# Gated DeltaNet tiles: decay matrix in its own buffer, a tile's output finished after the next tile's Gram products, v copied unscaled, no state work in tile 0; GLA output matmuls grouped by shape

## The chip, the cores and the metric

The kernel runs on one core of a Trainium2 chip. The metric is the device time of one execution in microseconds; three executions are known for the kernel before. Engines are named as in the profile: PE is the matmul engine (TensorE; PEld is its weight loads), DVE is VectorE, ACT is ScalarE, POOL is GpSimd, SP only issues DMAs.

## The reference

Two layers of `x + W_out[concat_g(mixer_g(h) * silu(z_g))]` with `h = RMSNorm(x)`, 512 tokens, width 2048. One input projection of 7192 columns feeds four mixers with 4 heads each: GLA, sliding-window attention, differential attention and gated DeltaNet (GDN). The change touches GDN and the output of GLA.

```python
# GDN, chunks of C = 64 tokens, d = 128
qc = l2_norm(ch(q)) * d ** -0.5 ; kc = l2_norm(ch(k)) ; vc = ch(v)
dec = jnp.cumsum(g, axis=-1)
dmask = jnp.where(tril, jnp.exp(dec_i - dec_j), 0.0)
M = jnp.where(strict, (kb @ kc.T) * dmask, 0.0)      # kb = kc * beta
Tm = inverse(M + eye)
u = Tm @ (vc * beta) ; w = Tm @ (kb * exp(dec))
...
def step(S, inp):
    v_new = u_n - w_n @ S
    o_n = qd_n @ S + qk_n @ v_new
    S = S * dl_n + ke_n.T @ v_new
# S starts at zero; then o = rms_norm(o, norm_g), times silu(z)
# GLA, chunks of 64:
o = a @ vc + q_dec @ S_prev                          # o_intra + o_inter
```

## The kernel before

**Projection as the carrier.** PE multiplies in a split form: each weight block is held as a rounded high half (`w_hi`, a DMA that POOL issues) and the rest (`w_lo`, computed by POOL in line 399). One step ("kt") of `project` (line 414) is 12 matmuls of 128x512 in line 438, three for each of four accumulators `acc[0..3]` in PSUM. A chunk of 512 columns is 16 such steps. After a chunk the four accumulators are read out by `take_out` (ACT, line 881), and the first matmul of the next chunk into `acc[b]` waits for `acc_free`.

**Mixer work between projection steps.** The mixers are Python generators; at fixed places inside a chunk (`k`, `b` odd) `project` takes one stage of a generator. So the order of PE's instructions is written out: no scheduler moves anything. GDN has four tiles of 128 tokens (`t` = 0..3), 18 stages each, spread as 8 stages in chunk `dz` and 16 in each of `bz`, `az`, `aq`, `av`. Stages of one tile on PE:
- stage 1: `gap` (line 486: the decay matrix `AG` times a triangle, into PSUM bank 3) and `nat` (line 490: transposes of q, k, v into banks 0, 1, 2);
- stage 2: the Gram products `kk`, `kq` (line 498);
- stages 3 to 14: six levels of the triangular inverse, each a `y` stage (line 506) and a `q` stage (line 522). Between them ACT copies Y (line 994) and DVE updates X (line 1361);
- stages 15 to 18: the last blocks of the inverse and the state products `ks`, `qs` (line 541), then `pt`, `tr`, and `s`, `o` (lines 562, 565).

**ACT and DVE** run the same tiles in their own program order, tied by counting semaphores (`Steps`). For each tile ACT does squares (982, 983), the exponential of the decays (984), Ln and Exp for the norms (986 to 989, each with a table load ahead), the six copies, the gate, and at the end the output's square (1010), Ln and Exp (1012, 1014). `GDN_STAGES` also sets where ACT's `take_out` calls stand among its stages: after 8, 24, 40, 56 and 72. DVE computes `ke`, `red`, `cq`, `nb`, `ei`, `nt0..3`, `qk`, then `r` (line 1351, v times 1/norm), `xi` (line 1352, the identity into X), the levels, and at the end of the tile `o` (1383), `redo` (1385), `mo` (1387), the four output products `y0..3` (1391), and only then `decayed(t + 1)` (1328), which builds `AG` of the next tile. `AG` shares its place with `QK`, and the `o` products read `QK`:

```python
U = dict(..., KE=unit(9, 0), AG=unit(9, 1), QK=unit(9, 1), ...)
def decayed(t):
    if t:
        dve.wait_ge(D_PE.sem, D_PE.at(l, f"{t-1}.o"))
    dve.tensor_tensor(U["AG"], heads(after_all), cols(glog[:, t]), ALU.mult)
```

**GLA** has one tile per chunk in the four chunks after GDN, six stages each. Its last stage makes, for each head, one 128-row product (line 624) and two 64-row products (line 628) into the same PSUM columns.

Of the kernel before, what the change touches and what calls it, by code (L numbers as in the profile page):

```python
# [23 lines left out]
EPS = 1e-6  # L24
# [60 lines left out]
def names(fmt, *ranges):  # L85
# [10 lines left out]
GDN_PE = "gap nat kk kq y1 q1".split() + [f"{a}{lv}" for lv in LV for a in ("y", "tx", "q")] + \  # L96
    "fin y7 ks qs pt tr s o".split()
GDN_ACT = "sqq sqk ex lnk rk irk".split() + [f"y{lv}" for lv in range(1, LEVELS + 1)] + \
    "gate y7 tt0 tt2 sqo lno ro".split()
GDN_DVE = "ag ke red cq nb ei nt0 nt1 nt2 nt3 qk r xi x1".split() + [f"{a}{lv}" for lv in LV for a in ("xt", "x")] + \  # L100
    "tt1 g3 rn0 rn1 rn2 rn3 qs w s0 s1 s2 s3 o redo mo y0 y1 y2 y3".split()
# [17 lines left out]
def hybrid_trunk(nc, x, wstream, wsmall, pcol, prow, wlr, cf, masks, out):  # L119
    ctx = ExitStack()  # L120
    with ctx:
# [81 lines left out]
        U = dict(S=unit(8, 0), R=unit(8, 1), W=unit(8, 2), QS=unit(8, 3), KE=unit(9, 0), AG=unit(9, 1), QK=unit(9, 1),  # L203
# [75 lines left out]
        def lay(prefix, *parts):  # L279
# [11 lines left out]
                                                                    "glog", "gA", "zero_tt", "zero_gdn"] +  # L291
# [4 lines left out]
        D_PE = Steps(sem("gdn_pe"), names("", T, GDN_PE))  # L296
        D_ACT = Steps(sem("gdn_act"), names("", T, GDN_ACT))
        D_DVE = Steps(sem("gdn_dve"), names("", T, GDN_DVE))
# [107 lines left out]
        def _(pe):  # L406
# [47 lines left out]
            def gdn(l):  # L454
# [11 lines left out]
                for t in T:  # L466
# [87 lines left out]
                    dve_at("rn3")  # L554
# [14 lines left out]
            def gla(l, t):  # L569
# [51 lines left out]
                for h in H:  # L621
                    b, p = slice(DK * (h % 2), DK * (h % 2) + DK), h // 2
                    o = mh[3 if h % 2 else 1]
                    nc.tensor.matmul(o[:, h], V["AT"][:, h], slot(SLOT["av"])[:, t, HD * h:HD * h + HD],
                                     start=True, stop=False)
                    for j in range(2):
                        r = slice(CH * j, CH * j + CH)
                        last = nc.tensor.matmul(o[r, h], V["QKT"][b, P * p + CH * j:P * p + CH * j + CH],
                                                V["S"][b, (2 * t + j) % 3, p], start=False, stop=True)
# [240 lines left out]
        def _(act):  # L870
# [57 lines left out]
            for l in range(DEPTH):  # L928
# [13 lines left out]
                def conv_gate(c):  # L942
# [32 lines left out]
                    .then_inc(S_ACT.sem, S_ACT.one("decs"))  # L975
                def gdn():

                    for t in T:
# [5 lines left out]
                        nc.scalar.activation(U["EX"], mh[3], ACT.Exp).then_inc(*s("ex"))  # L984
                        w(D_DVE, "red")
# [4 lines left out]
                        yield  # L990
                        yield
# [190 lines left out]
        def _(dve):  # L1182
# [57 lines left out]
            for l in range(DEPTH):  # L1240
# [81 lines left out]
                dve.memset(U["S"], 0.0).then_inc(*si("zero_gdn"))  # L1322

                def decayed(t):

                    if t:
                        dve.wait_ge(D_PE.sem, D_PE.at(l, f"{t-1}.o"))
                    dve.tensor_tensor(U["AG"], heads(after_all), cols(glog[:, t]), ALU.mult) \
                        .then_inc(D_DVE.sem, D_DVE.one(f"{t}.ag"))

                decayed(0)
                for t in T:
# [6 lines left out]
                    dve.tensor_scalar(sc, ss[:, 0:4], EPS, EPS * HD, ALU.add, ALU.mult).then_inc(*s("cq"))  # L1339
# [11 lines left out]
                    dve.tensor_tensor(U["R"], mh[2], cols(rs[:, 8:12]), ALU.mult).then_inc(*s("r"))  # L1351
                    dve.tensor_copy(X, ident_half.unsqueeze(1).broadcast_to([P, HEADS, CH])).then_inc(*s("xi"))
                    w(D_DVE, "xi")
                    for lv in range(1, LEVELS + 1):
                        if lv > 1:
# [8 lines left out]
                            .then_inc(*s(f"x{lv}"))  # L1364
                    w(D_PE, "fin")
# [274 lines left out]
```

## Time and profile before

| what | value |
|---|---|
| median of 3 executions | 2056.3 us (2053.81 to 2058.85) |
| profiled execution, its own time | 2057.32 us |
| its span, first to last instruction | 2055.5 us |
| PE busy | 1969.5 us (96%) |
| DVE, ACT, POOL busy | 659.5, 518.3, 919.7 us |
| chain that ended last | PE 83% of the span, 68% in line 438 alone |
| mean granted TensorE clock | 0.984 of full speed |

The profiled execution's time is its span plus 1.8 us around it, and lies 1.0 us above the median. The busy time of PE counts matmuls whose ends are modelled; starts are what the text uses.

### The profile page before, as it was taken

How to read it: one execution, taken by the hardware profiler on the slowest of the kernel's cores; microseconds unless marked ns; L12 is line 12 of the kernel's file. 1: busy time of each engine (PE TensorE's matmuls, PEld its weight loads, DVE VectorE, ACT ScalarE, POOL GpSimd, SP SyncE). 2: the span in 40 equal slices, each digit the busy share in tenths (PEclk: the TensorE clock that was granted, in tenths of full speed). 3: DMA queues.
4: the chain of work that ended last, by engine and by line, in shares of the span. 5: the costliest groups of instructions: out<-in, count | busy, mean ns of one | idle time of the engine just before them, and what ended most of it. 6: DMA issues, size and time to landing. Idle time of an engine off the chain costs nothing.

```text
span 2055.5 us, 26277 instructions
## 1 busy us (share of the span) xinstructions
PE 1969.5 (96%) x10984; PEld 1586.3 (77%) x10984; DVE 659.5 (32%) x1252; ACT 518.3 (25%) x1014; POOL 919.7 (45%) x876
## 2 busy tenths in 40 slices
PE   7999988989999999999999999989999999999999
PEld 5887777777888878777888877777778887786787
DVE  1545123122111343443324462232221113425433
ACT  4111122022222444322321011221222225533220
POOL 4455433433555444344555544333434444433454
PEclk9999999999999999999999999999999999999999
DMA  8565544544555544645775655434445555464466
GB/s 273 156 189 166 146 118 120 144 123 124 164 164 164 164 139 144 209 133 160 216 222 155 194 154 144 123 112 135 135 129 165 165 164 162 127 213 128 151 172 197
DMA packets 92181, 326.95 MB, mean 159 GB/s; under 512 B 10174, under 2 KB 10912, under 8 KB 91040
## 3 DMA queue, kind: packets, MB, share of 16 engines
q0 software_dynamic: 41472, 151.01, 26.4%
q1 hardware_dynamic: 44288, 155.75, 25.4%
q10 hardware_dynamic: 6304, 18.52, 2.3%
q8 instruction: 87, 1.43, 0.3%
q14 instruction: 30, 0.25, 0.0%
HBM read 316.86 MB, written 8.39 MB: 158 GB/s over the span
## 4 chain that ended last, share of the span: by engine, by line
PE 83%; DVE 8%; ACT 7%; issue 1%; DMA 1%; SPq 0%; ACTq 0%; DVEq 0%
PE acc L438 68%; PE mix L710 1%; PE mix L490 1%; DVE slots L1288 1%; PE mix L506 1%; PE mix L522 1%; ACT L1074 1%; ACT L1071 1%; PE mix L729 1%; PE mix L541 1%; PE mix L688 1%; PE mix L802 1%; PE mix L512 1%; PE mix L757 1%; DMA slots<-in_x 1%
## 5 line engine op out<-in xcount | busy, mean ns | idle before, releaser
L399 POOL TENSOR_TENSOR w_lo<-w_raw,w_hi 128x512 fp32r<-128x512 f32 x576 | 754.3, 1310 | 790.6 <-DMA w_hi<-in_wstream 506.0
L438 PE MATMUL acc<-w_hi,actT_hi 128*128 128x512 f32 x1920 | 788.1, 410 | 9.8 <-ACT slots L881 9.3
L438 PE MATMUL acc<-w_hi,actT_lo 128*128 128x512 f32 x1920 | 754.5, 393 | 0.0
L438 PE MATMUL acc<-w_lo,actT_hi 128*128 128x512 f32 x1920 | 753.0, 392 | 0.0
L438 PEld LDWEIGHTS acc<-w_hi,actT_hi 128*128 128x128 f32 x1920 | 365.0, 190 | 101.1 <-issue 28.8
L438 PEld LDWEIGHTS acc<-w_hi,actT_lo 128*128 128x128 f32 x1920 | 362.7, 189 | 79.3
L438 PEld LDWEIGHTS acc<-w_lo,actT_hi 128*128 128x128 f32 x1920 | 365.2, 190 | 66.1
L381 POOL DMA_DIRECT2D w_hi<-in_wstream x288 | 163.7, 568 | 335.0 <-PE acc L438 330.8
L438 PE MATMUL acc<-actT_hi,w_hi 128*128 128x512 f32 x384 | 152.6, 397 | 0.0
L438 PE MATMUL acc<-actT_hi,w_lo 128*128 128x512 f32 x384 | 150.1, 391 | 0.0
L438 PE MATMUL acc<-actT_lo,w_hi 128*128 128x512 f32 x384 | 150.0, 391 | 0.0
L438 PEld LDWEIGHTS acc<-actT_hi,w_lo 128*128 128x128 f32 x384 | 72.4, 188 | 15.4
L438 PEld LDWEIGHTS acc<-actT_hi,w_hi 128*128 128x128 f32 x384 | 72.5, 189 | 15.0 <-issue 0.5
L438 PEld LDWEIGHTS acc<-actT_lo,w_hi 128*128 128x128 f32 x384 | 72.4, 189 | 14.9 <-issue 0.5
L994 ACT ACTIVATE slots<-mix 128x256 f32<-128x256 f32 x48 | 18.5, 385 | 250.4 <-PE mix L506 250.4
L1508 DVE TENSOR_TENSOR slots<-acc,slots 128x512 f32<-128x512 f32 x64 | 43.6, 692 | 88.6 <-PE acc L438 88.6
L948 ACT ACTIVATE general<-slots 128x512 f32<-128x512 f32 x24 | 15.2, 633 | 211.7 <-DVE slots L1288 211.7
L1288 DVE SCALAR_TENSOR_TENSOR slots<-slots,pcol_all 128x511 f32<-128x511 f32 (+2 forms) x72 | 67.2, 933 | 2.5
L1361 DVE COPY_PREDICATED slots<-mask_sb,mix 128x256 f32<-128x256 uint8 x48 | 21.5, 448 | 143.7 <-PE mix L522 143.7
L881 ACT ACTIVATE slots<-acc,xr 128x512 f32<-128x512 f32 x56 | 36.9, 688 | 90.8 <-PE acc L438 90.8
L1357 DVE COPY slots<-mix 128x256 f32<-128x256 f32 x40 | 17.0, 425 | 124.8 <-PE mix L512 124.8
L1404 DVE SCALAR_TENSOR_TENSOR slots<-mix,slots 128x256 f32<-128x256 f32 x8 | 3.4, 424 | 155.4 <-ACT slots L1032 155.4
(247 smaller groups left out, 1754.6 us busy)
## 6 DMA issues: line engine op xcount, KB each, us to landing
w_hi<-in_wstream POOLq DMA_DIRECT2D x288, 512.0 KB, 3.9
w_raw<-in_wstream SPq DMA_DIRECT2D x288, 512.0 KB, 4.5
out_x<-slots ACTq DMA_DIRECT2D x7, 1024.0 KB, 8.0
slots<-in_x SPq DMA_DIRECT2D x4, 1024.0 KB, 15.6
slots<-in_x ACTq DMA_DIRECT2D x1, 4096.0 KB, 16.8
slots<-out_x ACTq DMA_DIRECT2D x1, 4096.0 KB, 16.3
out_x<-slots ACTq DMA_DIRECT2D x4, 256.0 KB, 2.2
cf_sb<-in_cf ACTq DMA_DIRECT2D x1, 933.0 KB, 11.2
```

The source lines that it names most:

```text
L381: pool.dma_start(w_hi[:, g % HI].rearrange("p a n -> p (a n)"), wstream[g:g + 1].rearrange("a p n -> p (a n)")).then_inc(hi_in[g % HI], 16)
L399: pool.tensor_tensor(w_lo[:, n % RING], w_raw[:, g % RAW, k], w_hi[:, g % HI, k].bitcast(F32), ALU.subtract).then_inc(w_ready, 1)
L438: last = nc.tensor.matmul(acc[b][:, :], lhsT, rhs, start=(k == 0 and i == 0), stop=(k == kts - 1 and i == 2))
L490: last = nc.tensor.transpose(mh[i][:, h], s[:, h, cs], ident)
L506: last = nc.tensor.matmul(y_out[rs_, j, gs], U["NT"][js, h, js], X[js, h] if lv > 1 else ident_half[js, :], start=True, stop=True)
L512: last = nc.tensor.transpose(mix[1][:, P * g:P * g + P], X[:, 2 * g:2 * g + 2].rearrange("p h c -> p (h c)"), ident)
L522: last = nc.tensor.matmul(p_out[js, r, gs], XT[rs_, g, js] if lv > 1 else ident_half[rs_, :], Y[rs_, j, gs], start=True, stop=True)
L541: last = nc.tensor.matmul(mh[i][:, h], s[:, h, cs], U["S"][:, h], start=True, stop=True)
L881: nc.scalar.activation(slot(SLOT[c])[:, b], acc[b][:, :], ACT.Copy, scale=r) \
L1288: dve.scalar_tensor_tensor(dst[:, d:], src[:, 0:SEQ - d], tap[i], dst[:, d:], ALU.mult, ALU.add).then_inc(*ci(f"t{i}"))
L1361: dve.copy_predicated(X_by_r, m_x[lv - 1].rearrange("p (g c) -> p g c", g=2).unsqueeze(1) .broadcast_to([P, 2, 2, CH]), p_out.rearrange("p ...
L1508: dve.tensor_tensor(xs, acc[b][:, :], xs, ALU.add).then_inc(acc_free, 1)
```

## The change

- `AG` gets its own place (`unit(7, 0)`), and `decayed(t + 1)` is issued before the `w` step of tile t instead of after its output.
- The tail of a tile's output (`redo`, `mo`, `y0..3` on DVE; Ln and Exp on ACT) goes into `gdn_out(t)` and `out_scale(t)`, issued in the next tile: on DVE after `xi`, on ACT after the norms' Exp and before the first Y copy. For the last tile they stand behind all stages and, on ACT, behind `take_out` of `av`.
- ACT copies v out of PSUM unscaled (step `v`); DVE scales it (`r`) in SBUF after the first level. PE's first `y` stage waits for `xi` and `v`, before for `r`.
- Tile 0 has no `ks`, `qs` products and no state terms; the zeroing of S goes.
- GLA's last stage makes the four 128-row products first and then the eight 64-row ones.

```diff
-        U = dict(... KE=unit(9, 0), AG=unit(9, 1), QK=unit(9, 1),
+        U = dict(... KE=unit(9, 0), AG=unit(7, 0), QK=unit(9, 1),
...
-                        dve_at(f"x{lv-1}" if lv > 1 else "r")
+                        dve_at(f"x{lv-1}" if lv > 1 else "xi")
+                        if lv == 1:
+                            act_at("v")
...
-                    if t == 0:
-                        pe.wait_ge(S_DVE.sem, S_DVE.at(l, "zero_gdn"))
-                    for i, s, step in ((0, k, "ks"), (1, q, "qs")):
+                    for i, s, step in ((0, k, "ks"), (1, q, "qs")) if t else ():
...
                 for h in H:
+                    nc.tensor.matmul(mh[3 if h % 2 else 1][:, h], V["AT"][:, h],
+                                     slot(SLOT["av"])[:, t, HD * h:HD * h + HD], start=h < 2, stop=False)
+                for h in H:
                     b, p = slice(DK * (h % 2), DK * (h % 2) + DK), h // 2
                     o = mh[3 if h % 2 else 1]
-                    nc.tensor.matmul(o[:, h], V["AT"][:, h], slot(SLOT["av"])[:, t, HD * h:HD * h + HD],
-                                     start=True, stop=False)
...
+                def out_scale(t):
+
+                    act.wait_ge(D_DVE.sem, D_DVE.at(l, f"{t}.mo"))
+                    nc.scalar.activation(sa, sa, ACT.Ln).then_inc(D_ACT.sem, D_ACT.one(f"{t}.lno"))
+                    act.wait_ge(D_ACT.sem, D_ACT.at(l, f"{t}.lno"))
+                    nc.scalar.activation(sa, sa, ACT.Exp, scale=-0.5).then_inc(D_ACT.sem, D_ACT.one(f"{t}.ro"))
...
+                        nc.scalar.activation(U["R"], mh[2], ACT.Copy).then_inc(*s("v"))
...
                         yield
+                        if t:
+                            out_scale(t - 1)
                         yield
...
                     take_out(l, c)
+                out_scale(TILES - 1)
...
-                dve.memset(U["S"], 0.0).then_inc(*si("zero_gdn"))
...
-                    dve.tensor_tensor(U["R"], mh[2], cols(rs[:, 8:12]), ALU.mult).then_inc(*s("r"))
                     dve.tensor_copy(X, ident_half.unsqueeze(1).broadcast_to([P, HEADS, CH])).then_inc(*s("xi"))
+                    if t:
+                        gdn_out(t - 1)
...
+                        if lv == 1:
+                            dve.scalar_tensor_tensor(U["R"], U["R"], 1.0 if t else -1.0, cols(rs[:, 8:12]),
+                                                     ALU.mult, ALU.mult).then_inc(*s("r"))
...
+                    if t + 1 < TILES:
+                        decayed(t + 1)
                     w(D_PE, "tr")
                     dve.tensor_tensor(U["W"], mh[0], cols(sd), ALU.mult).then_inc(*s("w"))
...
+                    else:
+                        dve.tensor_copy(U["S"], mh[2]).then_inc(*s("s"))
...
-                    if t + 1 < TILES:
-                        decayed(t + 1)
+                gdn_out(TILES - 1)
```

What ACT's order is around the start of tile 3, layer 0, before (982 to 984 read the transposes; 986 to 989 are the norms with a table load ahead of each function; 881 is `take_out` of `aq`; 994 are the Y copies):

```order
L982 ACTIVATE slots<-mix 128x512
L983 ACTIVATE slots<-mix 128x512
L984 ACTIVATE general<-mix 128x512
L986 ACT_TABLE_LOAD
L986 ACTIVATE stat<-stat,eps_t 128x4
L988 ACT_TABLE_LOAD
L988 ACTIVATE stat<-stat 128x4
L989 ACTIVATE stat<-stat 128x4
L881 ACTIVATE slots<-acc,xr 128x512 x4
L994 ACTIVATE slots<-mix 128x256 x6
```

The same stretch of the changed kernel (1018 to 1020 are the old 982 to 984, 1021 is the copy of v, 1023 to 1026 the norms, 1008 and 1010 are `out_scale` of tile 2, 910 is `take_out`, 1033 the Y copies):

```order
L1020 ACTIVATE general<-mix 128x512
L1021 ACTIVATE slots<-mix 128x512
L1023 ACT_TABLE_LOAD
L1023 ACTIVATE stat<-stat,eps_t 128x4
L1025 ACT_TABLE_LOAD
L1025 ACTIVATE stat<-stat 128x4
L1026 ACTIVATE stat<-stat 128x4
L1008 ACT_TABLE_LOAD
L1008 ACTIVATE stat<-stat 128x4
L1010 ACT_TABLE_LOAD
L1010 ACTIVATE stat<-stat 128x4
L910 ACTIVATE slots<-acc,xr 128x512 x4
```

Ln and Exp of tile 2's output, with two table loads, now stand between tile 3's norms and the read-out of chunk `aq`.

DVE at the end of tile 1 and the start of tile 2, before (1376 is `w`, 1379 the state, 1383 `o`, 1385 `redo`, 1387 `mo`, 1391 `y0..3`, 1328 the next `AG`, 1336 and 1337 `ke` and `red` of the next tile):

```order
L1376 TENSOR_TENSOR slots<-mix,stat 128x512
L1379 SCALAR_TENSOR_TENSOR slots<-slots,decs,mix 128x128 x4
L1383 TENSOR_TENSOR slots<-mix,slots 128x512
L1385 TENSOR_REDUCE stat<-slots 128x4
L1387 SCALAR_TENSOR_TENSOR stat<-stat 128x4
L1391 SCALAR_TENSOR_TENSOR slots<-slots,stat 128x128 x4
L1328 TENSOR_TENSOR slots<-cf_sb,glog 128x512
L1336 TENSOR_TENSOR slots<-mix,decs 128x512
```

The same stretch of the changed kernel (1361 is the next `AG`, 1434 `w`, 1438 the state, 1445 `o`; 1385 to 1401 are the next tile's `ke` to `xi`; 1370, 1372, 1377 are `redo`, `mo`, `y0..3` of the tile before; 1412 is the first update of X):

```order
L1361 TENSOR_TENSOR slots<-cf_sb,glog 128x512
L1434 TENSOR_TENSOR slots<-mix,stat 128x512
L1438 SCALAR_TENSOR_TENSOR slots<-slots,decs,mix 128x128 x4
L1445 TENSOR_TENSOR slots<-mix,slots 128x512
...
L1401 COPY slots<-cf_sb 128x256
L1370 TENSOR_REDUCE stat<-slots 128x4
L1372 SCALAR_TENSOR_TENSOR stat<-stat 128x4
L1377 SCALAR_TENSOR_TENSOR slots<-slots,stat 128x128 x4
L1412 COPY_PREDICATED slots<-mask_sb,mix 128x2x2x64
```

`AG` has moved ahead of `w`, and the output's tail has moved from the end of its tile to behind `xi` of the next.

## Rows read from the trace of the kernel before

**Rows 1.** Waits of PE and of DVE: in total, times, longest, all in us.
```profile
PE mix L486 <- DVE slots L1328: 31.0, 8, 4.5
DVE slots L1376 <- PE mix L556: 51.0, 8, 6.4
```

**Rows 2.** Timeline of PE, tile 0 to 1, layer 0: start, length, what, idle before.
```profile
262.66 0.39 PE L438 MATMUL acc<-w_hi,actT_lo 128*128 128x512 f32 x1
267.57 1.51 PE L486 MATMUL mix<-cf_sb,slots 128*128 128x128 f32 x8 [4.52 <-DVE slots L1328]
268.87 2.77 PE L490 MATMUL mix<-cf_sb,slots 128*128 128x128 f32 x12
271.29 0.61 PE L438 MATMUL acc<-w_hi,actT_hi 128*128 128x512 f32 x1
...
279.73 0.46 PE L506 MATMUL mix<-cf_sb,slots 64*64 64x64 f32 x16 [0.78 <-DVE slots L1351]
```

**Rows 3.** Timeline of DVE, same stretch.
```profile
260.50 0.68 DVE L1383 TENSOR_TENSOR slots<-mix,slots 128x512 f32<-128x512 f32 x1
...
262.60 1.29 DVE L1387 SCALAR_TENSOR_TENSOR stat<-stat 128x4 f32<-128x4 f32 x1
...
266.74 0.68 DVE L1328 TENSOR_TENSOR slots<-cf_sb,glog 128x512 f32<-128x512 f32 x1
...
279.50 0.42 DVE L1352 COPY slots<-cf_sb 128x256 f32<-128x256 f32 x1
```

**Rows 4.** Windows: busy time (instructions) of PE, PEld, DVE, ACT, POOL; granted clock; DMA.
```profile
726.10:728.10 2.00, 2.00 (x13) 1.82 (x14) 0.83 (x4) 0.00 (x0) 0.88 (x1) 1.00 0.81 236
268.90:271.20 2.30, 2.30 (x12) 2.30 (x11) 0.00 (x0) 0.00 (x0) 0.00 (x0) 0.50 0.00 0
```

**Rows 5.** Timeline of PE: a short wait in layer 0's attention part.
```profile
726.10 1.13 PE L688 MATMUL mix<-slots 128*128 128x128 f32 x8 [1.28 <-DVE slots L1489]
```

**Rows 6.** Timeline of ACT and PE around the first take-out behind GDN.
```profile
486.22 0.63 ACT L1010 ACTIVATE slots<-slots 128x512 f32<-128x512 f32 x1 [8.85 <-DVE slots L1383]
...
490.55 2.41 ACT L881 ACTIVATE slots<-acc,xr 128x512 f32<-128x512 f32 x4
...
491.36 0.76 PE L438 MATMUL acc<-w_hi,actT_hi 128*128 128x512 f32 x1 [4.67 <-ACT slots L881]
...
496.61 0.51 PE L438 MATMUL acc<-w_hi,actT_hi 128*128 128x512 f32 x1
```

**Rows 7.** Chain that ended last: a long run of projection matmuls, start, length, count.
```profile
90.34 74.36 PE acc L438 x327
```

**Rows 8.** Timeline of PE: products ks and qs of tile 0, layer 0.
```profile
246.53 2.05 PE L541 MATMUL mix<-slots 128*128 128x128 f32 x16
```

**Rows 9.** Timeline of ACT, start of tile 1, layer 0.
```profile
273.27 1.28 ACT L986 ACT_TABLE_LOAD   x1
274.64 0.30 ACT L986 ACTIVATE stat<-stat,eps_t 128x4 f32<-128x4 f32 x1
```

**Rows 10.** Timeline of POOL at the end of tile 0, layer 0.
```profile
262.58 1.28 POOL L399 TENSOR_TENSOR w_lo<-w_raw,w_hi 128x512 fp32r<-128x512 f32 x1
```

**Rows 11.** Timeline of ACT and PE at the start of chunk av, tile 3.
```profile
426.41 2.40 ACT L881 ACTIVATE slots<-acc,xr 128x512 f32<-128x512 f32 x4
...
427.48 0.39 PE L438 MATMUL acc<-w_hi,actT_hi 128*128 128x512 f32 x1
```

**Rows 12.** Timeline of DVE and PE at the start of tile 0, layer 0.
```profile
191.12 0.48 DVE L1322 MEMSET slots<- 128x512 f32 x1
...
192.49 1.52 PE L486 MATMUL mix<-cf_sb,slots 128*128 128x128 f32 x8 [1.94 <-DVE slots L1328]
```

**Rows 13.** Timeline of PE: GLA tile 0, layer 0.
```profile
521.00 0.67 PE L615 MATMUL mix<-slots 64*64 64x128 f32 x16
...
527.18 0.38 PE L624 MATMUL mix<-slots,general 128*128 128x128 f32 x2
...
530.22 0.50 PE L438 MATMUL acc<-w_hi,actT_hi 128*128 128x512 f32 x1
```

More of the change, by code:

```diff
@@ L95, with gdn_pe, gdn_act, gdn_dve @@
 LV = range(2, LEVELS + 1)
[L96 to L101, printed above, removed]
+LV = range(2, LEVELS + 1)
+def gdn_pe(t):
+    return "gap nat kk kq y1 q1".split() + [f"{a}{lv}" for lv in LV for a in ("y", "tx", "q")] + ["fin", "y7"] + \
+        (["ks", "qs"] if t else []) + "pt tr s o".split()
+def gdn_act():
+    out = []
+    for t in T:
+        out += [f"{t}.{x}" for x in "sqq sqk ex v lnk rk irk".split()]
+        if t:
+            out += [f"{t-1}.lno", f"{t-1}.ro"]
+        out += [f"{t}.y{lv}" for lv in range(1, LEVELS + 1)] + [f"{t}.{x}" for x in "gate y7 tt0 tt2 sqo".split()]
+    return out + [f"{TILES-1}.lno", f"{TILES-1}.ro"]
+def gdn_dve():
+    end = "redo mo y0 y1 y2 y3".split()
+    out = ["0.ag"]
+    for t in T:
+        out += [f"{t}.{x}" for x in "ke red cq nb ei nt0 nt1 nt2 nt3 qk xi".split()]
+        if t:
+            out += [f"{t-1}.{x}" for x in end]
+        out += [f"{t}.x1", f"{t}.r"] + [f"{t}.{a}{lv}" for lv in LV for a in ("xt", "x")] + [f"{t}.tt1", f"{t}.g3"]
+        if t:
+            out += [f"{t}.{x}" for x in "rn0 rn1 rn2 rn qs".split()]
+        if t + 1 < TILES:
+            out += [f"{t+1}.ag"]
+        out += [f"{t}.w"] + ([f"{t}.s{h}" for h in range(3)] if t else []) + [f"{t}.s", f"{t}.o"]
+    return out + [f"{TILES-1}.{x}" for x in end]
 GLA_PE = "u cum dec tr a us o".split()
@@ L295, in hybrid_trunk @@
         CONV_ACT = Steps(sem("conv_act"), [f"{c}{b}" for c in ("dq", "dk", "dv") for b in range(4)])
-        D_PE = Steps(sem("gdn_pe"), names("", T, GDN_PE))
-        D_ACT = Steps(sem("gdn_act"), names("", T, GDN_ACT))
-        D_DVE = Steps(sem("gdn_dve"), names("", T, GDN_DVE))
+        D_PE = Steps(sem("gdn_pe"), [f"{t}.{x}" for t in T for x in gdn_pe(t)])
+        D_ACT = Steps(sem("gdn_act"), gdn_act())
+        D_DVE = Steps(sem("gdn_dve"), gdn_dve())
         A_PE = Steps(sem("gla_pe"), names("", T, GLA_PE))
@@ L1321, in _, with gdn_out @@
                 dve.memset(U["TT"], 0.0).then_inc(*si("zero_tt"))
-                dve.memset(U["S"], 0.0).then_inc(*si("zero_gdn"))
                 def decayed(t):
-                    if t:
-                        dve.wait_ge(D_PE.sem, D_PE.at(l, f"{t-1}.o"))
                     dve.tensor_tensor(U["AG"], heads(after_all), cols(glog[:, t]), ALU.mult) \
                         .then_inc(D_DVE.sem, D_DVE.one(f"{t}.ag"))
+                def gdn_out(t):
+                    w = lambda st, s: dve.wait_ge(st.sem, st.at(l, f"{t}.{s}"))
+                    s = lambda step: (D_DVE.sem, D_DVE.one(f"{t}.{step}"))
+                    gz = slot(SLOT["dz"])[:, t].rearrange("p (h c) -> p h c", h=HEADS)
+                    w(D_ACT, "sqo")
+                    dve.reduce_sum(ss[:, 8:12], U["SQO"], AX.X).then_inc(*s("redo"))
+                    w(D_DVE, "redo")
+                    dve.scalar_tensor_tensor(sa, ss[:, 8:12], 1.0 / HD, (sc, se)[t % 2], ALU.mult, ALU.add) \
+                        .then_inc(*s("mo"))
+                    w(D_ACT, "ro")
+                    w(D_DVE, "g3")
+                    for h in H:
+                        dve.scalar_tensor_tensor(gz[:, h], U["QS"][:, h], sa[:, h:h + 1], gz[:, h],
+                                                 ALU.mult, ALU.mult).then_inc(*s(f"y{h}"))
                 decayed(0)
```

55 lines of the change are left out of this document (26 added, 29 removed).

## The prediction

> **What bounds the kernel now.** The profile's first part says that PE is busy for 96% of the span and DVE, ACT and POOL for less than half, and the chain that ended last is 83% PE. So PE's own program sets the time, and an edit counts only if it takes instructions from PE or changes how long PE waits or at which clock it runs. I therefore read PE's waits next. The largest is line 486, the first product of a GDN tile, behind DVE's line 1328, which builds `AG`: 31.0 us in 8 waits [rows 1]. The timeline shows one of the six between tiles: last projection matmul at 262.66, next PE instruction at 267.57 [rows 2]. What PE waits for there is the whole tail of tile 0 on DVE and ACT: `o` done at 261.18, `mo` at 262.60, the new `AG` from 266.74 [rows 3]. The time is more than the 4.52 us of idleness, because the clock falls: the products and transposes behind the wait run at a granted 0.50, that is 1.2 GHz [rows 4]; behind the wait of 1.28 us at 726.10 [rows 5] it stays at 1.00 [rows 4]. The same happens once per layer behind GDN: PE waits 4.67 us for ACT to read out chunk `av`, which stands behind the output's Ln and Exp, and the next twelve wide matmuls take from 491.36 to 496.61 [rows 6], 5.25 us, where twelve at full clock take 12 x 74.36/327 = 2.73 [rows 7].
>
> **Between tiles (t = 1, 2; both layers).** I count from c, the start of the last projection matmul before the tile (262.66). Before, the first `y` stage starts at 279.73 = c + 17.1 [rows 2]. After, `AG` is long there: DVE makes it in the gap ahead of `w`, where it waits 6.4 us for PE in every tile [rows 1], so its 0.68 us [rows 3] cost nothing; without that gap they would be 0.68 per tile. PE also waits for `o` of the tile before; it ended at 261.18 [rows 3] and PE is ready at c + 0.23 = 262.89, so 1.7 us to spare. Stage 1 then runs at full clock: 8 products at the rate of `ks`, `qs` (16 in 2.05 us, 0.24 of it the modelled end of the last [rows 8]), 0.9 us, and 12 transposes in half of what they took at clock 0.50, (271.29 - 268.87)/2 = 1.21 [rows 2]. The next projection matmul starts at f = c + 2.34.
>
> From f to the first `y` stage the chain is ACT and DVE, not PE: before, 279.73 - 271.29 = 8.44. The copy of v delays the norms' table load by its issue distance of 0.5 us; the Ln behind it started at 274.64 though its table was there at 274.55 [rows 9], so 0.4 of it comes through. `r` leaves the chain: -0.60 (a 128x512 operation of 0.68 whose successor starts 0.60 later). But PE now waits for the end of `xi`, 279.92, where it waited for `r`, about 279.58: +0.34 [rows 3]. Sum +0.14, so 8.6, and `y1` starts at c + 10.95 instead of c + 17.1. Gain 6.1 us per tile, four tiles: **-24.5**. PE still waits some 1.2 us ahead of `y1`; going by [rows 4, 5] the clock stays up.
>
> **The tail in its new place.** On DVE: `xi` ends at about f + 8.5, `redo` 0.7, `mo`. `mo` took 1.29 us [rows 3] although it is 128x4; POOL's `w_lo` subtraction ran from 262.58 to 263.86 [rows 10], and `mo` ended at 263.89. The Trainium skill (SBUF — State Buffer, "SBUF: two separate sides") says that a DVE operation with two SBUF inputs and a GpSimd operation exclude each other for a whole instruction; the trace agrees. By the page `mo` would be short here only if no `w_lo` subtraction runs. The rows leave about 0.2 (my estimate; on ACT an operation of this size takes 0.30 [rows 9]) to 1.29. I take 0.2, since a subtraction of 1.28 per projection step of 2.73 leaves POOL's port free for more than half of the time, and keep the other end. Then Ln 0.2, table load 1.28 [rows 9], Exp 0.2: done at f + 11.05. The Ln's own table load passes while ACT waits. The first Y copy ends at f + 11.4; PE wants it one stage after `y1`, f + 8.6 + 3.3 = f + 11.9 (twelve wide matmuls and 16 small ones). So no wait, or 0.6 per tile with the long `mo`: 0 to +2.5, taken 0. `y0..3` (1.1 us) end by f + 13.3 at worst; X's first update is wanted at f + 15.2. Covered; without cover 1.1 per tile.
>
> **Tile 3.** Here the order of ACT matters: `take_out` of chunk `aq` comes behind the 56th stage, and there `out_scale(2)` now stands ahead of it. Before, the read-out began at 426.41 and its first 0.69 ended before PE wanted `acc[0]` at 427.48 [rows 11]; queued behind it are PE's whole next chunk and the `y` stage. Now: Exp ends f + 11.05, the first of four read-outs (0.6 to 0.7) f + 11.65, PE gets on at f + 11.8. It was ready at f + 2.7 + 1.7 + 1.4 = f + 5.9 (12 matmuls, 16 products, 6 matmuls): a new wait of about 5.9 us. It is longer than the 4.67 of [rows 6], so I let 12 wide matmuls run at half clock as there. Six of them (2.6) stand before `y1`: f + 14.4 = c + 16.75, before about c + 17.0; and the rest of the slow stretch adds 1.4. Tile 3 so gains nothing: +1.1 per layer, **+2.2**. Bounds: +1.1 more per layer with the long `mo`, 1 less if the clock comes back sooner.
>
> **Tile 0.** PE waits 1.94 us for the memset of S and `AG` behind it [rows 12]; the memset's 0.48 go. A wait of 1.45 is nearer to the 1.28 that kept the clock than to 1.94, which did not keep it. If it is kept, stage 1 takes 2.1 instead of about 3.7 (as from 267.57 to 271.29 [rows 2]). 0.5 + 1.6 less 0.14 is 1.9 per layer, bounds 0.3 and 1.9; I take 1.7: **-3.4**. `ks` and `qs` go: 2.05 - 0.24 - 0.1 for the turn back = 1.7 per layer [rows 8]: **-3.4**.
>
> **Behind GDN.** ACT's `take_out` of `av` now follows the square that ends at 486.85 [rows 6]. Its first read-out of 0.69 ends at 487.54, PE starts 0.12 later (as 491.36 stands to 490.55 + 0.69), and the twelve matmuls end by 490.5 instead of 496.61: 6.1 per layer, **-12.2**. If the remaining wait of 1.1 us still brings the half clock, 2.5 less per layer. The last `out_scale` then waits for the read-out and two table loads, and its `y3` ends about 493.5, some 2 us later than before; GLA's first product, which waits for it, stands 36 projection matmuls in, at 487.7 + 8.2 = 495.9. Covered by 2.4 us; without cover up to 2 per layer.
>
> **GLA output.** The last stage runs from 527.18 to 530.22 [rows 13], 3.04 us for 8 + 16 instructions. Ordered by shape, the eight take 0.9 and a turn of 0.1, and 16 of 64 rows take 0.6, as line 615 does just before with the same kind (0.67 with its modelled end) [rows 13]. 1.45 per tile, 8 tiles: **-11.5**. The other end is that the narrow ones keep their present pace of 0.36 per four: -0.7 each, -5.5.
>
> **Sum.** -24.5 + 2.2 - 3.4 - 3.4 - 12.2 - 11.5 = -52.8 against the profiled execution's 2057.3 us: 2004.5. The median of three lies 1.0 lower: **2003.5 us**.
>
> **Rivals.**
> - *The clock.* The waits of 1.2 us ahead of `y1`, with no long gap between tiles any more, are followed by half clock: twelve matmuls at double time, 2.5 us, in 6 places: +15, 2018.5. For it: 1.94 was enough. Against: 1.28 was not. Chance 0.12.
> - *Tile 3 escapes.* PE's wait for the read-out is hidden and tile 3 gains like tiles 1 and 2: -14.4, 1989. Against it: the order shown on ACT leaves no way round, and ACT's Ln cannot start before `xi`. Chance 0.04.
> - *A slower switch of tables.* Each table load holds ACT for another length of itself: +1.3 at tile 3's read-out, +0.8 at each first Y copy: +5.8, 2009. Against: Ln started 0.09 after its load's end [rows 9]. Chance 0.04. The Trainium skill (ScalarE: Activation LUTs, "What ACT_TABLE_LOAD costs") has such a rule, a drain of about 1.38 us with each load; in this trace it does not show.
> - *Slower than before.* PE falls to half clock at the wait ahead of `y1` and stays there through the inverse's levels, whose small products and short waits fill it less than before. Every wide matmul at half clock costs 0.2 us; it decides from 52.8/0.2 = 264 of them, 33 in each of 8 tiles (a tile has 216). All of them would give +340, half a tile each +170, about 2175. Against: before, the same levels ran at full clock, and at 0.984 on average. Chance 0.03.
> - *Nothing happens*, since PE still waits for `o` of the tile before: it had 1.7 us to spare. Then only tile 0, the end and GLA count. Within 0.3% needs more failures still: 0.02.
>
> **How the numbers follow.** My forecast has 0.75, with its own range 1996 to 2011. The slower table switch (2009) lies in it; to 2017 it takes in part of the clock's case. Range 1995 to 2017. Differences under 0.3% (6 us) count as none. Faster 0.95, same 0.02, slower 0.03.
>
> **What would show it.** PE's waits: line 486 behind DVE gone for t > 0, about 1.4 us left for t = 0; a wait of about 1.2 us ahead of each `y1` but tile 3's; two new waits of 5 to 7 us for `take_out` in chunk `av`, clock 0.50 behind them; the wait of 4.67 us down to about 1.1. GLA's last stage 1.6 us. The prediction is wrong if half clock follows short waits, or if the narrow GLA products keep their pace.

## The result, and the profile after

| | before | after |
|---|---|---|
| median of four executions | 2056.84 us (2053.81 to 2058.85) | 2000.89 us (1998.3 to 2004.94) |
| profiled execution, its time | 2057.32 us | 2004.94 us |
| its span | 2055.5 us | 2002.9 us |
| mean granted TensorE clock | 0.984 | 0.993 |

The ratio after to before is 0.9731, 95% interval 0.9708 to 0.9754: the changed kernel is 2.7% faster. The forecast was 2003.5 us. The profiled execution is the slowest of its four; the tables below go by it, and its forecast was 2004.5 us.

The page of the changed kernel, parts 1 and 4: busy time by engine, and the chain that ended last by engine.

```profile
PE 1938.3 (97%) x10952; PEld 1564.2 (78%) x10952; DVE 652.0 (33%) x1234; ACT 521.7 (26%) x1022; POOL 921.4 (46%) x876
...
PE 85%; ACT 7%; DVE 6%; issue 1%; DMA 1%; SPq 0%; ACTq 0%; DVEq 0%
```

PE's waits after, in the columns of [rows 1] (total, times, longest). Line numbers have moved: 466 is the projection (438 before), 514 the `gap` products (486), 536 the first `y` stage (506), 910 ACT's `take_out` (881), 717 an attention product (688), 739 another (710).

```profile
PE acc L466 <- ACT slots L910: 13.0, 4, 5.6
PE mix L717 <- DVE slots L1543: 11.0, 6, 2.7
PE mix L739 <- DVE slots L1577: 7.5, 2, 3.8
PE mix L536 <- DVE slots L1401: 6.7, 6, 1.1
PE mix L514 <- DVE slots L1361: 5.2, 2, 2.8
```

Line 486's 31.0 us in 8 waits [rows 1] are 5.2 us in 2: only the tiles t = 0 still wait there. Six waits of 1.1 us stand ahead of `y1`. ACT's `take_out` is waited for four times, twice at 5.6 us and twice at 0.88.

PE's timeline between tiles 0 and 1 of layer 0 after (start, length, what, idle before), which answers to [rows 2]:

```profile
262.06 0.39 PE L466 MATMUL acc<-w_hi,actT_lo 128*128 128x512 f32 x1
262.29 1.05 PE L514 MATMUL mix<-cf_sb,slots 128*128 128x128 f32 x8
263.17 1.47 PE L518 MATMUL mix<-cf_sb,slots 128*128 128x128 f32 x12
264.40 0.48 PE L466 MATMUL acc<-w_hi,actT_hi 128*128 128x512 f32 x1
...
273.06 0.46 PE L536 MATMUL mix<-cf_sb,slots 64*64 64x64 f32 x16 [1.12 <-DVE slots L1401]
```

There is no wait ahead of `gap`, and the transposes run at full clock (1.47 us where they took 2.77 [rows 2]). `y1` starts at c + 11.0, where c is 262.06; the prediction had c + 10.95.

PE at tile 3 of layer 0 after, from the first projection matmul behind stage 1 (f = 402.37) on:

```profile
402.37 0.48 PE L466 MATMUL acc<-w_hi,actT_hi 128*128 128x512 f32 x1
...
414.14 0.77 PE L466 MATMUL acc<-w_hi,actT_hi 128*128 128x512 f32 x1 [5.60 <-ACT slots L910]
...
416.97 0.71 PE L536 MATMUL mix<-cf_sb,slots 64*64 64x64 f32 x16
...
419.48 0.46 PE L466 MATMUL acc<-w_lo,actT_hi 128*128 128x512 f32 x1
```

ACT in the same stretch (1008 and 1010 are the output's Ln and Exp of tile 2, 910 the read-outs of chunk `aq`):

```profile
411.70 0.20 ACT L1008 ACTIVATE stat<-stat 128x4 f32<-128x4 f32 x1 [2.46 <-DVE stat L1372]
411.93 1.28 ACT L1010 ACT_TABLE_LOAD   x1
413.22 0.20 ACT L1010 ACTIVATE stat<-stat 128x4 f32<-128x4 f32 x1
413.33 2.41 ACT L910 ACTIVATE slots<-acc,xr 128x512 f32<-128x512 f32 x4
```

The read-out stands behind an Exp that has nothing to do with it. PE gets on at f + 11.77 (predicted f + 11.8) after 5.60 us of idleness (predicted 5.9), and wide matmuls then start 0.43 us apart instead of 0.23 until 419.48. Granted clock, in the columns of [rows 4]: behind this wait, behind the read-out of `av` (tile 3 is done there), and behind a `y1` wait of 1.12.

```profile
414.20:416.80 2.60, 2.60 (x6) 1.74 (x6) 0.40 (x2) 1.54 (x3) 0.00 (x0) 0.50 0.06 24
476.10:480.00 3.90, 3.90 (x17) 3.23 (x18) 1.31 (x1) 3.85 (x6) 1.90 (x2) 1.00 0.78 200
273.10:276.00 2.90, 2.90 (x27) 2.42 (x28) 1.07 (x3) 1.97 (x4) 0.72 (x1) 1.00 0.91 247
```

Behind GDN, PE after, where [rows 6] had a wait of 4.67 and half clock:

```profile
476.07 0.47 PE L466 MATMUL acc<-w_hi,actT_hi 128*128 128x512 f32 x1 [0.88 <-ACT slots L910]
```

And GLA's last stage of tile 0, layer 0, after, which answers to [rows 13]:

```profile
509.36 1.05 PE L650 MATMUL mix<-slots,general 128*128 128x128 f32 x8
510.34 0.67 PE L657 MATMUL mix<-slots 64*64 64x128 f32 x16
510.94 0.50 PE L466 MATMUL acc<-w_hi,actT_hi 128*128 128x512 f32 x1
```

From the first product to the next projection matmul it is 510.94 - 509.36 = 1.58 us, where it was 3.04.

**Where the time came from.** The stretches below lie between the same instructions in both profiled executions; each is the difference of two starts. The last row but one is what the others leave of the span.

| stretch | before | after | change | predicted |
|---|---|---|---|---|
| tiles 1, 2: `s` of the tile before to `y1`, four times | 21.36, 21.31, 21.90, 21.90 | 15.30, 15.30, 15.29, 15.30 | -25.3 | -24.5 |
| tile 3: `s` of tile 2 to `s` of tile 3, twice | 74.93, 74.93 | 76.14, 75.96 | +2.2 | +2.2 |
| tile 0: last projection matmul ahead of `gap` to `y1`, twice | 14.50, 13.93 | 15.22, 15.67 | +2.5 | -3.4 |
| tile 0 without `ks`, `qs`: `y1` to `s`, twice | 53.71, 53.70 | 51.90, 51.91 | -3.6 | -3.4 |
| behind GDN: `s` of tile 3 to GLA's first product, twice | 18.90, 18.92 | 12.57, 12.53 | -12.7 | -12.2 |
| GLA: its last stage to the next tile's first product, counted for 8 tiles | 26.38 | 24.92 | -11.7 | -11.5 |
| the rest of the span | | | -4.0 | 0 |
| span | 2055.5 | 2002.9 | -52.6 | -52.8 |

### The profile page after: what moved, and what is told of

Read it like the earlier page. It is cut to its first block, busy times and chain, and to the rows that moved or that the text cites. A ratio compares the mean times of both kernels' runs of the same rounds, so it can differ in the third digit from the quotient of the medians.

```text
span 2002.9 us, 26201 instructions
## 1 busy us (share of the span) xinstructions
PE 1938.3 (97%) x10952; PEld 1564.2 (78%) x10952; DVE 652.0 (33%) x1234; ACT 521.7 (26%) x1022; POOL 921.4 (46%) x876
## 4 chain that ended last, share of the span: by engine, by line
PE 85%; ACT 7%; DVE 6%; issue 1%; DMA 1%; SPq 0%; ACTq 0%; DVEq 0%
PE acc L466 71%; DVE slots L1324 1%; PE mix L739 1%; PE mix L536 1%; PE mix L552 1%; ACT L1110 1%; ACT L1107 1%; PE mix L758 1%; PE mix L831 1%; PE mix L542 1%; PE mix L786 1%; PE mix L717 1%; PE mix L518 1%; DMA slots<-in_x 1%; PE mix L569 1%
## 5 line engine op out<-in xcount | busy, mean ns | idle before, releaser
L1189 ACT ACTIVATE slots<-mix 128x512 f32<-128x512 f32 (+3 forms) x32 | 14.0, 439 | 138.0 <-PE mix L749 138.0
```

## The experiments

Each ratio is to the kernel before, run on the same chip; medians are of four executions, and of seven for the kernel before. The sets ran on different chips, so between sets the ratios are the better measure.

### First set: the parts alone, and the order at tile 3

These four ran together; the kernel before had 2057.71 us (2052.97 to 2060.18).

**e1_ag_only**: the kernel before, with nothing but `AG` in its own place and made ahead of `w`. The whole tail stays at the end of its own tile.

```diff
-        U = dict(... AG=unit(9, 1), ...
+        U = dict(... AG=unit(7, 0), ...
...
-                    if t:
-                        dve.wait_ge(D_PE.sem, D_PE.at(l, f"{t-1}.o"))
...
+                    if t + 1 < TILES:
+                        decayed(t + 1)
                     w(D_PE, "tr")
...
-                    if t + 1 < TILES:
-                        decayed(t + 1)
```

> The kernel before with one edit: AG has its own place and is built ahead of the w step; the output's tail (redo, mo, Ln, Exp, y0 to y3) stays at the end of its tile. My theory: PE's 4.5 us ahead of each tile, and the half clock behind them, come from the shared buffer alone. The tail then runs beside stage 1: ACT's Exp ends at 265.65 and the squares could start at 265.4, so the chain to y1 is late by 0.3 us only. PE's wait at line 486 is gone in all six places, the wait ahead of y1 is about 1.3, tile 3 gains too (nothing stands ahead of the read-out of aq): 6 times 6 us, some 37 us with layer 1's longer slow stretches, about 2020 us. The wait of 4.67 for the read-out of av stays. Rival: the tail has to leave the end of the tile as well, since the next tile's squares on ACT and ke on DVE queue behind it; then the wait moves to y1 at 4 to 5 us there, and the time is about 2044 us.

Measured: 2017.52 us (2016.1 to 2018.32), ratio 0.9808 (0.9792 to 0.9824). PE around the start of tile 1 and ACT in the same stretch (1026 is the output's Exp, 994 the square of q):

```profile
262.33 0.39 PE L450 MATMUL acc<-w_hi,actT_lo 128*128 128x512 f32 x1
...
273.33 0.46 PE L518 MATMUL mix<-cf_sb,slots 64*64 64x64 f32 x16 [1.12 <-DVE slots L1361]
```

```profile
265.11 0.20 ACT L1026 ACTIVATE stat<-stat 128x4 f32<-128x4 f32 x1
265.22 0.58 ACT L994 ACTIVATE slots<-mix 128x512 f32<-128x512 f32 x1
```

The tail does stand ahead of the squares on ACT, and `y1` still starts at c + 11.0 (273.33 - 262.33), as in the changed kernel. So the tail's move was not needed for the gain between tiles. `AG` in its own place, and so made earlier, was enough: 40.2 us (interval 36 to 43), where 37 were expected. That is more than the 22.3 (24.5 less 2.2) that the changed kernel was to gain there, since here tile 3 gains as well: 6 x 6.1 = 36.6.

**e2_gla_only**: the kernel before with the GLA products grouped, and their start and stop flags set for that order.

```diff
+                for h in H:
+                    nc.tensor.matmul(mh[3 if h % 2 else 1][:, h], V["AT"][:, h], ...)
                 for h in H:
                     b, p = slice(DK * (h % 2), DK * (h % 2) + DK), h // 2
```

> The kernel before with GLA's last stage in the new order and nothing else. My theory: the stage falls from 3.04 to 1.6 us in 8 tiles, so 11.7 us less, about 2045 us, because the turns between 128-row and 64-row products go from 8 to 2. Rival: what costs is that each narrow product adds to columns just written; then some of it stays and the stage takes 2.3 us, 6 us less, about 2051 us.

Measured: 2043.65 us (2041.17 to 2045.0), ratio 0.9935 (0.9917 to 0.9952), that is -9.9 to -17.1 us. The predicted -11.5 lies in it, the other end (-5.5) does not. In its trace the last stage takes 1.58 us in all eight tiles, as in the changed kernel. Why the old order cost more is not shown: the new one has fewer turns between the two shapes, and also no narrow product any more that adds to columns written just before it, and no run separates the two.

**e3_readout_first**: the changed kernel, with ACT's `take_out` of `aq` ahead of tile 2's Ln and Exp.

```diff
-                        if t:
+                        if t and t + 1 < TILES:
                             out_scale(t - 1)
                         yield
+                        if t + 1 == TILES:
+                            out_scale(t - 1)
```

> The changed kernel, but in tile 3 ACT's take_out of chunk aq stands ahead of the Ln and Exp of tile 2's output. My theory: the two waits of 5.6 us for that read-out, with the half clock behind them, are all that tile 3 lost; both go, PE waits about 1.1 us ahead of y1 of tile 3 as in the others, and the time falls by 2 times 7.2, 14 us, to about 1987 us. The first Y copy of tile 3 still comes in time (it ends some 0.4 us before PE wants it). Rival: the read-out's 2.4 us on ACT then push Ln and Exp back and the wait moves to the first q stage, 2 us or more of it; then about 1992 us or above.

Measured: 1989.85 us (1988.01 to 1991.7), ratio 0.9674 (0.9658 to 0.9691). Its waits of PE:

```profile
PE mix L536 <- DVE slots L1403: 8.2, 8, 1.1
...
PE acc L466 <- ACT slots L910: 1.8, 2, 0.9
```

and ACT and PE at tile 3, layer 0:

```profile
405.75 2.41 ACT L910 ACTIVATE slots<-acc,xr 128x512 f32<-128x512 f32 x4
...
411.25 0.37 ACT L1035 ACTIVATE slots<-mix 128x256 f32<-128x256 f32 x1
```

```profile
408.94 0.46 PE L536 MATMUL mix<-cf_sb,slots 64*64 64x64 f32 x16 [0.75 <-DVE slots L1403]
...
412.32 0.46 PE L552 MATMUL mix<-slots,cf_sb 64*64 64x64 f32 x16
```

Both 5.6 us waits are gone, and nothing new took their place: the Y copy at 411.25, now behind the Exp, still ends before PE wants it at 412.32. By the medians the two waits and their half clock are worth 2000.89 - 1989.85 = 11 us. In the traces, `s` of tile 2 to `s` of tile 3 falls from 76.14 and 75.96 to 69.04 and 68.99, 14.1 us, beside the 14.4 that the prediction gave as the worth of an escape.

**e4_last_readout**: the kernel before, with only the last tile's Ln and Exp behind `take_out` of `av`.

```diff
-                        w(D_DVE, "mo")
-                        nc.scalar.activation(sa, sa, ACT.Ln)...
+                        if t + 1 < TILES:
+                            scale_out(t)
...
                     take_out(l, c)
+                scale_out(TILES - 1)
```

> The kernel before with one edit: behind the last GDN stage ACT's take_out of chunk av stands ahead of the last tile's Ln and Exp. My theory: the wait of 4.67 falls to 0.9 and the clock stays up, 6.3 us per layer as in the changed kernel, 12.7 us less, about 2044 us. Rival: the wait was only part of it, and GLA's first product, which waits for the last y3, takes it back: then 0 to 4 us less, above 2052 us.

Measured: 2043.06 us (2042.3 to 2044.12), ratio 0.9933 (0.9914 to 0.9952). PE's wait for `take_out`, 9.3 us in 2 before, in its trace:

```profile
PE acc L438 <- ACT slots L881: 1.8, 2, 0.9
```

That is the term behind GDN, alone: one change of order on ACT per layer, 14.6 us (interval 9.9 to 17.7; predicted 12.2). In its trace `s` of tile 3 to GLA's first product takes 12.57 and 12.53 us, as in the changed kernel, so the later `y3` held nothing up.

### Second set: tile 0, and what the tail and v do

Run together; the kernel before had 2056.86 us (2053.89 to 2059.86).

**e5_first_decay_early**: e3 and, for tile 0, `AG` made before the last convolution, with the memset of `TT` behind it.

```diff
+                decayed(0)
                 turned_out("dv")
                 conv("dv", T)
                 dve.memset(U["TT"], 0.0).then_inc(*si("zero_tt"))
...
-                decayed(0)
```

> On top of the kernel with the read-out first (take_out of aq ahead of tile 2's Ln and Exp): AG of tile 0 is built ahead of the last of the three convolutions, and the memset of TT comes behind it, where PE does not wait for it. My forecast had tile 0's wait fall to 1.45 us with the memset gone; it was 2.36 and 2.82. Theory: PE waits there for memset and AG at the end of DVE's queue, AG stretched to 1.35 us by POOL's subtraction; with both out of the way the wait is for the last convolution alone, 0.6 to 1.3 us, the clock stays up, and the time falls by 2 times 3.4 us to about 1983 us. Rival: DVE's convolutions themselves are late by the same stretching, so the wait falls by 0.5 us only, the half clock stays, and the time is about 1989 us.

Measured: 1983.48 us (1982.86 to 1984.81), ratio 0.9645 (0.963 to 0.9659). PE at tile 0, layer 0:

```profile
190.70 1.13 PE L514 MATMUL mix<-cf_sb,slots 128*128 128x128 f32 x8
191.67 1.47 PE L518 MATMUL mix<-cf_sb,slots 128*128 128x128 f32 x12
```

No wait is left here (0.09 us in layer 1), where 0.6 to 1.3 were expected, and the transposes run at full clock. By the medians it is 6.4 us for the two layers, some 3.2 each: the wait of about 2 and the clock behind it. The edit takes both `AG` and a memset out of PE's way; it does not say what each is worth.

**e6_tail_home**: e5 with the tails of tiles 0 to 2 back at the end of their own tiles, on ACT and DVE.

```diff
-                        if t:
-                            out_scale(t - 1)
...
+                        if t + 1 < TILES:
+                            out_scale(t)
...
-                    if t:
-                        gdn_out(t - 1)
...
+                    gdn_out(t)
```

> The kernel with tile 0's AG early, but for tiles 0 to 2 the output's tail (redo, mo, Ln, Exp, y0 to y3) back at the end of its own tile; only the last tile's Ln and Exp stay behind take_out of av. If moving the tail is worth nothing once AG has its own place, as the AG-only kernel suggests (the next tile's squares started 0.2 us late there), the time is within 2 us of the kernel it is compared with. If the tail's new place is worth something, this one is slower by 6 times the wait that appears ahead of y1, 3 us for each 0.5.

Measured: 1982.54 us (1981.66 to 1984.09), ratio 0.9641 (0.9624 to 0.9657). That is within noise of e5: where the tail stands is worth nothing that can be measured, as long as it stands ahead of no read-out.

**e7_v_scaled**: e5 with v scaled by DVE on its way out of PSUM again, ahead of `xi`, and no copy on ACT.

```diff
-                        if lv == 1:
-                            act_at("v")
...
-                        nc.scalar.activation(U["R"], mh[2], ACT.Copy).then_inc(*s("v"))
...
+                    dve.scalar_tensor_tensor(U["R"], mh[2], 1.0 if t else -1.0, cols(rs[:, 8:12]),
+                                             ALU.mult, ALU.mult).then_inc(*s("r"))
                     dve.tensor_copy(X, ident_half...
```

> The kernel with tile 0's AG early, but v is scaled out of PSUM by DVE ahead of xi again and PE's first y stage waits for that, with no copy of v on ACT. By my sum the copy cost 0.4 us on ACT and the new wait for xi 0.34, against 0.6 gained on DVE: this one is faster by 0.14 us in each of 8 tiles, 1 us in all, which the timing cannot tell; in the trace the wait ahead of y1 is 1.0 instead of 1.1 us. If v leaving PSUM unscaled is where part of the gain lies, it is slower by 0.5 us per tile or more, 4 us.

Measured: 1982.3 us (1980.56 to 1985.73), ratio 0.964 (0.9624 to 0.9656). The waits ahead of `y1` in e7:

```profile
PE mix L534 <- DVE slots L1401: 6.4, 8, 0.8
```

In e5 they are 8.3 us in 8, the longest 1.1. That is 1.9 us less of waiting over eight tiles; the two times can't be told apart. In the traces `y1` starts at f + 8.66 in e5 and at f + 8.33 in e7, so the copy of v makes the chain 0.3 us longer: what `r` took off it was less than the copy and the wait for `xi` put on.

### Third set: the wait that was left

Run together; the kernel before had 2053.74 us (2052.19 to 2062.41). The first `y` stage multiplies `NT` by the identity from the constants. It reads no X, so the last thing that it needs is `nt3` (bank 2 must be read out too, which the wait for `v` sees to).

**e8_first_y_early**: e5, with that wait. **e9_home_and_early**: e6, with that wait.

```diff
-                        dve_at(f"x{lv-1}" if lv > 1 else "xi")
+                        dve_at(f"x{lv-1}" if lv > 1 else "nt3")
```

> The kernel with tile 0's AG early, and PE's first y stage waits for nt3, the last operand that it reads, instead of xi, two operations further on DVE's queue (and for the copy of v, as before). The wait of 1.12 ahead of y1 is for qk and xi alone, 1.2 us of DVE. My theory: it goes nearly in all 8 tiles. But in tiles 1 and 2 the first Y copy stands behind tile t-1's Ln and Exp on ACT, which end at the same time as before; PE then wants it at 7.5 + 3.3 = 10.8 us behind f where it can have it at 11.4, so 0.6 us come back ahead of the first q stage, more in tile 3 where the read-out pushes them back. Gain 8 times 1.1 less 4 times 0.6 less 2 times 0.5: 5 us, about 1978 us. If it does not matter what y1 waits for, because the chain behind it is the same, 1983 us.

> The kernel with the output's tail at the end of its own tile, and y1 waiting for nt3. Here nothing stands ahead of the first Y copy on ACT, so the whole 1.1 us per tile is kept: 8 us less than 1982.5, about 1974 us, and no new wait ahead of the first q stage. If my reading of the tail's new place is wrong, it is no faster than the kernel with the tail in the next tile.

Measured: e8 1976.13 us (1975.39 to 1977.64), ratio 0.9616 (0.9595 to 0.9637); e9 1975.03 us (1974.7 to 1979.12), ratio 0.9609 (0.9585 to 0.9633). PE's waits in e8, where the one ahead of `y1` is gone and a shorter one for the Y copy behind Ln and Exp has come:

```profile
PE mix L552 <- ACT slots L1035: 2.5, 6, 0.5
```

In e9, where ACT makes that copy at once, it does not exist; there PE waits for the read-outs at the ends of `aq` and `av`:

```profile
PE acc L464 <- ACT slots L908: 2.5, 4, 0.9
```

By the medians both gain 7.4 us over e5 and e6; by the ratios it is 6.0 and 6.6 us. In the traces the tiles' own stretches are 5.2 us shorter in e8 (5 were forecast) and 6.9 in e9 (8 were forecast). The forecasts lay 4 us apart, 1978 and 1974; the two medians can't be told apart. Either is the best version found, 3.8% to 3.9% under the kernel before and about 1.2% under the changed one.

e9's trace also shows that e5's edit does not always clear tile 0: in layer 0 PE waits 1.55 us ahead of `gap`, until the last convolution is done (191.75, PE at 191.85). Three of that convolution's operations took 3.22 us, where they take 2.32 undisturbed. The clock stayed at 1.00.

## Why the prediction was right, and where not

**Tiles 1 and 2: right.** Predicted -24.5, measured -25.3, and `y1` stands at c + 11.0 instead of c + 10.95. e1 shows the cause alone. What the prediction left open is shown too: the tail's new place (e6) has no part in it, and the copy of v (e7) costs 0.3 us per tile. One cause was overlooked: the +0.34 for waiting for `xi` rests on a row in which a POOL subtraction runs beside it. In both traces `xi` ends 0.15 to 0.17 us behind such a subtraction in all eight tiles, and in e1, in six tiles without one beside it, it took 0.28.

**Tile 3: right, term and mechanism.** It was +2.2 as predicted, with a wait of 5.60 us and clock 0.50 behind it. e3, which changes nothing but that place in ACT's order, brings 11 us. The short `mo` was also right: it took 0.16 us in six of its eight places, the six ahead of a next tile.

DVE and POOL after at tile 3, layer 0 (1401 is `xi`, 1372 `mo`, 427 `w_lo`'s subtraction):

```profile
409.44 1.28 POOL L427 TENSOR_TENSOR w_lo<-w_raw,w_hi 128x512 fp32r<-128x512 f32 x1
410.29 0.59 DVE L1401 COPY slots<-cf_sb 128x256 f32<-128x256 f32 x1
...
411.51 0.16 DVE L1372 SCALAR_TENSOR_TENSOR stat<-stat 128x4 f32<-128x4 f32 x1
```

**Behind GDN, `ks` and `qs`, GLA: right.** -12.7, -3.6 and -11.7 for -12.2, -3.4 and -11.5. The wait of 4.67 became 0.88 (predicted 1.1) and kept the clock. For GLA the time is right and its cause is not shown (e2).

**Tile 0: the step that failed.** The prediction took the memset's 0.48 us off PE's wait, and let the wait of 1.45 that was left keep the clock: -3.4. Measured +2.5. The waits were 2.36 and 2.82, and both were followed by half clock. POOL and DVE before, layer 0 (399 is `w_lo`'s subtraction, 1328 `AG`):

```profile
190.51 1.28 POOL L399 TENSOR_TENSOR w_lo<-w_raw,w_hi 128x512 fp32r<-128x512 f32 x1
```

```profile
191.52 0.82 DVE L1328 TENSOR_TENSOR slots<-cf_sb,glog 128x512 f32<-128x512 f32 x1
```

and after:

```profile
191.42 1.28 POOL L427 TENSOR_TENSOR w_lo<-w_raw,w_hi 128x512 fp32r<-128x512 f32 x1
```

```profile
191.49 0.48 DVE L1357 MEMSET slots<- 128x512 f32 x1
191.90 1.35 DVE L1361 TENSOR_TENSOR slots<-cf_sb,glog 128x512 f32<-128x512 f32 x1
```

`AG` ends at 192.34 before and 193.25 after, each time 0.55 us behind the end of POOL's subtraction (191.79, 192.70). Started 0.54 earlier behind its convolution, `AG` only took 0.53 longer. So in layer 0 taking the memset away brought nothing; it lay beside the subtraction. The Trainium skill (SBUF — State Buffer, "SBUF: two separate sides") has the rule that explains it, the one that the prediction used for `mo` and not for `AG`: a DVE operation with two SBUF inputs and a GpSimd operation that reads SBUF exclude each other; the trace agrees, by the 0.55 us of both kernels. e3, whose tile 0 is that of the changed kernel, says the same: `AG` 1.36 us long there, and a wait of 1.92, as before.

That the waits grew comes from the convolution ahead. In layer 0 its last operation ended 0.36 us behind the start of PE's last matmul before (190.52, 190.16) and 0.79 after (191.44, 190.65). In layer 1 it was 0.34 before (1207.11, 1206.77) and 1.98 after (1182.30, 1180.32); there the memset did come off (`AG` took 0.62), and more was lost than it gave. Three of the convolution's operations took 3.30 us where they had taken 2.32:

```profile
1177.17 3.30 DVE L1324 SCALAR_TENSOR_TENSOR slots<-slots,pcol_all 128x511 f32<-128x511 f32 x3
```

```profile
1178.64 1.29 POOL L427 TENSOR_TENSOR w_lo<-w_raw,w_hi 128x512 fp32r<-128x512 f32 x1 [2.46 <-DMA w_hi<-in_wstream]
```

The last of the three started at 1178.74, took 1.73 us instead of 0.75 and ended at 1180.47, again 0.55 behind the subtraction (1179.92). When that subtraction runs against the convolution is no part of the change, and it differs from trace to trace: the second waits of e3 and e1 are 2.21 and 2.48. No run moves it alone. Of the +2.5, 1.5 lie ahead of f; the other 1.0 lies between f and `y1` (9.05 and 8.81 where the forecast had 8.6), where PE waits for `xi`, stretched to 0.88 and 0.64 in the same way.

The prize at that place was larger than the forecast's: e5 takes the whole wait away and gains 6.4 us, where the prediction gave 3.4 for a part of the wait and the clock.

**The rest of the span: -4.0, not forecast, and luck.** It pays back most of tile 0's miss of 5.9 us; with it the profiled execution came out at -52.6 for -52.8. The median moved by 56, since the changed kernel's profiled execution lies 4.0 us above its median (granted clock 0.993, and 0.995 in the fastest); no trace shows why. Most of it is one wait of 2.72 us per layer in the attention part, before (two layers):

```profile
751.89 2.88 PE L688 MATMUL mix<-slots 128*128 128x128 f32 x16 [2.72 <-DVE slots L1489]
...
1769.01 2.83 PE L688 MATMUL mix<-slots 128*128 128x128 f32 x16 [2.73 <-DVE slots L1489]
```

and after:

```profile
728.24 2.02 PE L717 MATMUL mix<-slots 128*128 128x128 f32 x16 [2.72 <-DVE slots L1543]
...
1718.23 2.02 PE L717 MATMUL mix<-slots 128*128 128x128 f32 x16 [2.72 <-DVE slots L1543]
```

The windows behind the first of each, before and after, in the columns of [rows 4]:

```profile
752.00:756.00 4.00, 4.00 (x20) 3.71 (x21) 1.13 (x4) 0.00 (x0) 0.00 (x0) 0.61 0.38 119
```

```profile
728.30:732.30 4.00, 4.00 (x26) 3.62 (x27) 1.13 (x4) 0.00 (x0) 0.47 (x1) 1.00 0.32 109
```

The same wait ahead of the same products is followed by a granted 0.61 in one kernel and 1.00 in the other. From the products' start to the seventh projection matmul behind them it is 4.86 and 4.85 before, 3.25 and 3.25 after: -3.2. Two longer waits there, for line 1523 (1577 after), went from 4.50 and 3.84 to 3.81 and 3.70: -0.8. Why the clock fell in the one and not in the other is open: the change touches nothing in that part. Over the eleven kernels the products behind this wait ran at full clock 8 times of 22. All 8 are in the changed kernel and those made from it (8 of 14), none in the kernel before and those made from it (0 of 8); whether the change shifts the odds no run shows. It is in any case not a gain to be counted on: e9's two waits were both followed by half clock (3.54 and 3.52 us for the 16) and e8's both by full (2.02), and e9's profiled span is 3.2 us longer (1977.1, 1973.9) though its median is not.

**The rivals.** *The clock* (2018.5) did not come: the waits of 1.12 ahead of `y1` were followed by full clock, as in the window at 273.10. *Tile 3 escapes* (1989) needed another order on ACT; with it, e3 measured 1989.85. That this is the rival's number is in part chance, since e3 has tile 0's miss and the gain in the attention part in it too. *A slower switch of tables* (2009) did not show: Exp followed its load's end by 0.01 us (411.93 + 1.28, 413.22). *Slower than before* and *nothing happens*: the small stages of the inverse ran at full clock, and PE did not wait for `o` of the tile before.

## What to carry to other kernels

When an engine's program order is fixed, look at what stands ahead of each PSUM read-out in its queue: here a 0.2 us Exp with its wait and table load held the matmul engine for 4.7 us twice in the kernel before and for 5.6 us twice in the changed one, and each pair, moved, gave 11 to 15 us. When a buffer is shared, ask what its second user waits for: the decay matrix in a place of its own, and made earlier, was 40 us, and the rearranged tail that came with it nothing. Let PE wait for the last operand that it reads (`nt3`), not for the last instruction of the block that makes it ready (`xi`): 6 to 7 us. And before you take an operation's time off a wait, see what else runs beside the one behind it: that next operation can take up the time again.

## What the runs showed of the hardware

- Several kinds of DVE operation ended a fixed time behind a POOL subtraction that ran beside them. `AG` took 0.82 us before and 1.35 after (0.62 without one), its end 0.55 us behind POOL's both times; `mo` (128x4) 1.29 us beside a subtraction [rows 3, 10] and 0.16 without one; the copy `xi`, with one SBUF input, 0.42 to 0.93 beside one, its end 0.15 to 0.17 behind in all 16 places of the two kernels, and 0.28 in six places of e1 without. Work ahead of such an operation on DVE can be free, and taking it away can bring nothing.
- Waits of PE and the clock: those of 0.88, 1.12, 1.28 and 1.50 us were followed by a granted 1.00; one of 5.60 by 0.50, until 5.3 us after its end (414.14 to 419.48). In between the same wait went both ways: behind 1.92 us ahead of tile 0's products the twelve transposes took 1.47 us in e2 and 2.34 in e1, and the 2.72 us above was followed by either.
- Products of 128 and of 64 rows that alternate every two to four instructions took 3.04 us for 24, and in two runs of one shape each 1.58. Whether it is the turns that cost was not tested.
